# Two thirds of each down projection as seven products for eight, with sums of weights and activations on VectorE

## The reference, cut to what matters

```python
def swiglu(x, w_gate, w_up, w_down):
    return (jax.nn.silu(x @ w_gate) * (x @ w_up)) @ w_down
for l in range(DEPTH):                       # DEPTH = 2, D_FF = 2816, D_MODEL = 1024
    x = layer_norm(ALPHA * x + 0.5 * swiglu(x, ffn1...[l]), ...)
    x = layer_norm(ALPHA * x + mixer(x) @ w_out[l], ...)
    x = layer_norm(ALPHA * x + 0.5 * swiglu(x, ffn2...[l]), ...)
```

## Time and profile before

| | us |
|---|---|
| median of 3 runs | 3002.32 (3001.02 to 3002.56) |
| the profiled execution, span | 3005.2 |
| PE busy | 2914.0 (97%) |
| DVE busy | 1376.5 (46%) |
| ACT busy | 1024.2 (34%) |
| mean granted TensorE clock | 0.991 |

### The profile page before, as it was taken

The page is one execution under the profiler, slowest core; times in us unless marked ns, Lnnn a source line. Parts: engine busy times, 40 slices in busy tenths (PEclk is TensorE's granted clock), DMA queues, the critical chain, the costliest instruction groups (busy, mean ns, idle before and its releaser), DMA issues.

```text
span 3005.2 us, 34010 instructions
## 1 busy us (share of the span) xinstructions
PE 2914.0 (97%) x14625; PEld 2422.2 (81%) x14625; DVE 1376.5 (46%) x1931; ACT 1024.2 (34%) x1360; POOL 77.4 (3%) x91
## 2 busy tenths in 40 slices
PE   7999998999999989999999999999999999999998
PEld 7878887887888878888876888888888886788887
DVE  4345357734535663333556443334433364644235
ACT  4322443432234332222535422224222254542122
POOL 0010000001000000000100000000000100000000
PEclk9999999999999999999999999999999999999999
DMA  5222222322221222222521223232322351223222
GB/s 211 74 94 74 71 72 83 96 70 71 85 84 56 71 92 98 98 98 98 100 98 57 80 90 114 96 103 93 113 98 98 112 100 57 71 98 112 98 98 84
DMA packets 41318, 275.88 MB, mean 92 GB/s; under 512 B 5508, under 2 KB 5698, under 8 KB 9936
## 3 DMA queue, kind: packets, MB, share of 16 engines
q1 hardware_dynamic: 36064, 254.82, 25.0%
q0 software_dynamic: 4288, 15.22, 2.4%
q10 hardware_dynamic: 816, 3.67, 0.3%
HBM read 269.50 MB, written 2.10 MB: 90 GB/s over the span
## 4 chain that ended last, share of the span: by engine, by line
PE 91%; DVE 5%; ACT 2%; issue 1%; DMA 1%; DVEq 0%; ACTq 0%
PE G L395 16%; PE G L397 16%; PE G L396 16%; PE G L407 11%; PE G L409 11%; PE G L408 11%; DVE w_lo L1506 1%; PE A L902 1%; PE A L582 1%; PE A L924 1%; PE A L683 1%; PE A L912 1%; PE A L700 1%; DMA x<-in_x 1%; PE A L670 1%
## 5 line engine op out<-in xcount | busy, mean ns | idle before, releaser
L1506 DVE TENSOR_TENSOR w_lo<-raw,w_hi 128x2048 fp32r<-128x2048 f32 (+1 forms) x234 | 533.1, 2278 | 793.4 <-ACT w_hi L1006 792.9
L395 PE MATMUL G<-xT_hi,w_hi 128*128 128x512 f32 (+1 forms) x2368 | 881.0, 372 | 14.6 <-DVE x L2063 4.8
L397 PE MATMUL G<-xT_hi,w_lo 128*128 128x512 f32 (+1 forms) x2368 | 870.5, 368 | 0.0
L396 PE MATMUL G<-xT_lo,w_hi 128*128 128x512 f32 (+1 forms) x2368 | 869.8, 367 | 0.0
L1006 ACT ACTIVATE w_hi<-raw 128x2048 fp32r<-128x2048 f32 (+1 forms) x234 | 443.8, 1896 | 959.1 <-PE G L409 523.2
L395 PEld LDWEIGHTS G<-xT_hi,w_hi 128*128 128x128 f32 x2368 | 449.1, 190 | 87.0 <-DVE x L2063 5.2
L397 PEld LDWEIGHTS G<-xT_hi,w_lo 128*128 128x128 f32 x2368 | 448.9, 190 | 73.1
L396 PEld LDWEIGHTS G<-xT_lo,w_hi 128*128 128x128 f32 x2368 | 449.5, 190 | 68.8
L407 PE MATMUL G<-w_hi,h_hi 128*128 128x512 f32 x704 | 274.8, 390 | 1.0 <-DVE w_lo L1506 1.0
L409 PE MATMUL G<-w_hi,h_lo 128*128 128x512 f32 x704 | 274.0, 389 | 0.0
L408 PE MATMUL G<-w_lo,h_hi 128*128 128x512 f32 x704 | 273.9, 389 | 0.0
(11 more groups left out here) (297 smaller groups left out, 2984.1 us busy)
## 6 DMA issues: line engine op xcount, KB each, us to landing
raw<-in_stream SPq DMA_DIRECT2D x240, 1024.0 KB, 4.8
lnr<-in_ln_rows POOLq DMA_DIRECT2D x6, 1024.0 KB, 5.1
row<-in_rows POOLq DMA_DIRECT2D x6, 512.0 KB, 7.7
x<-in_x ACTq DMA_DIRECT2D x1, 2048.0 KB, 17.8
...
```

Source lines behind the costliest of these rows:

```text
L395: mm(o, a, hi[:, c, at:at + n], start=start and own_start, stop=False, **k)
L396: mm(o, a, lo[:, c, at:at + n], start=False, stop=False, **k)
L397: return mm(o, wl[:, col:col + P], hi[:, c, at:at + n], start=False, stop=stop, **k)
L1506: tt(w_lo[:, s, 0:nk, :], raw[:, r, 0:nk, :], w_hi[:, s, 0:nk, :].bitcast(F32), ALU.subtract).then_inc(lo_done, 1)
```

## The change

In each feed-forward the 11 units fall in parts of 4, 4 and 3. The down projections of the first two parts, 1024 hidden columns each, are no longer 4 tiles x 8 chunks x 2 halves. The 512 x 1024 activations and the 1024 x 1024 weights are taken as 2 x 2 quarters, and the result is made from seven products of quarters (256 tokens x 512 hidden x 512 outputs, 24 matmuls of 512 columns) in place of eight, in Winograd's form. Each product has a left side, h or one of four sums of h, and a right side, a quarter of the weights or one of four sums.

DVE makes the sums of h in each unit, in `work`, and ACT and DVE split them into `hs`, which has seven variants of 256 tokens. The quarters of weights are loaded by SP with alternate chunks (`alternate`, two loads of 0.5 MB each in 2 KB pieces), into the ring and a second buffer `raw2`; one quarter is loaded twice. DVE makes the sums of weights in place, two before the last unit's multiplications and two behind them. Then each of seven right sides is split like a block. The products go to banks 0 and 1, or 2 and 3, of G in turn; DVE adds each to `x` when it is done (`read_product`), and some accumulate upon the one before in the same bank.

In the last unit before the products ACT copies the block of product 0, then that of product 1, and then takes the two Silus; DVE subtracts both, makes two sums of weights, and then multiplies.

The third part of 3 units has 6 chunks, in blocks of 4 and 2 for each half, with new hand-written orders. The residuals of the norm before are done two in each of units 1 and 2. GpSimd's memset of `shift_t`, which now shares memory with `raw2`, waits for the first feed-forward's products.

```diff
-UNITS2 = 2 * (11 + 4) + 5 + 2
-FF_HALVES = ((6, (4, 4, 4)), (5, (4, 4, 2)))
-OUT2 = sum(2 * units + 2 * len(downs) for units, downs in FF_HALVES) + 10
+UNITS2 = 2 * (11 + 2) + 5 + 2
+SUMMED = 2
+LAST_DOWN = (4, 2)
+FF_HALVES = ((4, (4, 4)), (4, (4, 4)), (3, LAST_DOWN))
+FF_PARTS = tuple(units for units, _ in FF_HALVES)
+PRODUCTS = 7
+FF_BLOCKS = 2 * sum(FF_PARTS) + 4 * SUMMED + 2 * len(LAST_DOWN)
+OUT2 = FF_BLOCKS + 10
+SPLITS2 = BLOCK2 + 2 * SUMMED * (PRODUCTS - 4)
+RING2 = BLOCK2 - 2 * SUMMED * 2
+LEFT = (0, 1, 4, 3, 5, 6, 2)
+QUARTER = ((0, 0), (0, 0), (0, 1), (1, 1), (1, 1), (0, 1), (1, 0))
...
+        hs = sb("hs", [P, 4, 2, 7, 256], F32R, on=two)
+        with ExitStack() as over:
+            w3_hi = sb("w3_hi", [P, 2, BC], F32R, on=over)
+            w3_lo = sb("w3_lo", [P, 2, BC], F32R, on=over)
+        raw2 = sb("raw2", [P, 2, KB, BC], on=two)
...
+            def alternate(place, b, odd, signals):
+
+                for o in range(2):
+                    sp.dma_start(place[:, 2 * o:2 * o + 2, :],
+                                 stream[b + o:b + o + 1].rearrange("o p (k e n) -> (o p) k e n", e=2, n=BC)[:, :, odd, :]
+                                 ).then_inc(signals[o], 16)
+
+            def feed_forward(b, parts_before):
+
+                for n, units in enumerate(FF_PARTS):
+                    for i in range(2 * units):
+                        ring(b + i)
+                    b += 2 * units
+                    if n == SUMMED:
+                        for i in range(2 * len(LAST_DOWN)):
+                            ring(b + i)
+                        continue
+                    first = Q.split
+                    if parts_before + n == 0:
+                        sp.wait_ge(S["ln_c"], 1)
+                    alternate(raw2[:, 0], b + 2, 1, (raw2_in[0], raw2_in[0]))
+                    alternate(raw2[:, 1], b, 1, (raw2_in[1], raw2_in[1]))
+                    slot_free()
+                    alternate(raw[:, 0], b, 0, (half_in[0], raw_in[0]))
+                    taken(first + 4)
+                    slot_free()
+                    alternate(raw[:, 1], b + 2, 0, (half_in[1], raw_in[1]))
+                    taken(first + 3)
+                    sp.wait_ge(lo_done, first + 2 + 3)
+                    sp.wait_ge(S["w_sum"], 4 * (parts_before + n) + 4)
+                    alternate(raw2[:, 0], b + 2, 1, (raw2_in[0], raw2_in[0]))
+                    Q.split += PRODUCTS
+                    b += 4
...
+            def products(units):
+
+                for k in range(PRODUCTS):
+                    s, a = (Pos.off + Pos.turn) % 2, 2 * (k % 2)
+                    pe.wait_ge(lo_done, 2 * Pos.pair + Pos.off + 3)
+                    for i in range(2):
+                        if k < 2:
+                            pe.wait_ge(g_free[a + i], Pos.ubase + Pos.u + 1)
+                        else:
+                            pe.wait_ge(S["st_read"], N.st + 2 * (k - 2) + i + 1)
+                        o = G[:, a + i, :]
+                        for u in range(units):
+                            if i == 0:
+                                pe.wait_ge(S["ff_lo"], N.ff + 3 * u + min(k, 2) + 1)
+                            hi, lo = (hs[:, u, part, LEFT[k], i * P:i * P + P] for part in range(2))
+                            new, end = u == 0 and k in (0, 1, 3), u == units - 1
+                            mm(o, hi, w_hi[:, s, u, :], start=new, stop=False, skip_group_check=True)
+                            mm(o, hi, w_lo[:, s, u, :], start=False, stop=False, skip_group_check=True)
+                            last = mm(o, lo, w_hi[:, s, u, :], start=False, stop=end, skip_group_check=True)
+                        last.then_inc(blk_used if i else S["st_done"], 1)
+                    Pos.off += 1
+                N.st += 2 * PRODUCTS
+                Pos.held.update({0: N.st - 1, 1: N.st, 2: N.st - 3, 3: N.st - 2})
...
-            FF_ORDER = ((0, 0, 0, 4), (0, 1, 0, 4), (0, 2, 0, 4), (0, 3, 0, 4), (1, 0, 0, 4), (2, 0, 0, 2), (1, 1, 0, 4),
-                        (2, 1, 0, 2), (1, 2, 0, 4), (1, 3, 0, 2), (1, 3, 2, 4), (2, 2, 0, 2), (2, 3, 0, 2))
-            FF_LAST_ORDER = ((0, 0, 0, 4), (0, 1, 0, 4), (1, 0, 0, 4), (2, 0, 0, 2), (1, 1, 0, 4), (2, 1, 0, 2), (0, 2, 0, 4),
-                             (1, 2, 0, 4), (2, 2, 0, 2), (0, 3, 0, 4), (1, 3, 0, 4), (2, 3, 0, 2))
+            FF_ORDER = ((0, 0, 0, 4), (0, 1, 0, 4), (1, 0, 0, 2), (1, 1, 0, 2), (0, 2, 0, 4), (0, 3, 0, 2), (0, 3, 2, 4),
+                        (1, 2, 0, 2), (1, 3, 0, 2))
+            FF_LAST_ORDER = ((0, 0, 0, 4), (1, 0, 0, 2), (0, 1, 0, 4), (1, 1, 0, 2), (0, 2, 0, 4), (1, 2, 0, 2), (0, 3, 0, 4),
+                             (1, 3, 0, 2))
...
+
             def ffn(L, bias_rows=None):
-                for n, (units, downs) in enumerate(FF_HALVES):
+                for n, units in enumerate(FF_PARTS):
                     for u in range(units):
+                        before_products = n < SUMMED and u == units - 1
+                        if before_products:
+                            act.wait_ge(half_in[0], 16 * (N.parts + 1))
                         split()
+                        if before_products:
+                            act.wait_ge(raw2_in[1], 32 * (N.parts + 1))
+                            split_summed(raw2[:, 1])
+                        act.wait_ge(S["ff_lo"], N.ff)
                         for i in range(2):
 
                             done(i)
                             act.wait_ge(g_free[2 + i], Pos.ubase + Pos.u + 1)
                             fn(work[:, i * 512:i * 512 + 512], G[:, i, :], ACT.Silu).then_inc(g_free[i], 1)
-                        for i in range(2):
-                            act.wait_ge(g_free[2 + i], Pos.ubase + Pos.u + 2)
-                            fn(h_hi[:, 2 * u + i, :], work[:, 1024 + i * 512:1536 + i * 512],
+                        if n < SUMMED:
+                            act.wait_ge(g_free[2], Pos.ubase + Pos.u + 2)
+                            fn(hs[:, u, 0, 0, :], work[:, 1024:1280], ACT.Copy).then_inc(S["ff_hi"], 1)
+                            act.wait_ge(g_free[3], Pos.ubase + Pos.u + 2)
+                            fn(hs[:, u, 0, 1:3, :], work[:, 1536:2048].rearrange("p (a t) -> p a t", a=2),
                                ACT.Copy).then_inc(S["ff_hi"], 1)
-                        split()
+                            N.sums += 1
+                            act.wait_ge(S["ff_sum"], N.sums)
+                            fn(hs[:, u, 0, 3:7, :], work[:, 0:1024].rearrange("p (a t) -> p a t", a=4),
+                               ACT.Copy).then_inc(S["ff_hi"], 1)
+                            N.ff += 3
+                        else:
+                            for i in range(2):
+                                act.wait_ge(g_free[2 + i], Pos.ubase + Pos.u + 2)
+                                fn(h_hi[:, 2 * u + i, :], work[:, 1024 + i * 512:1536 + i * 512],
+                                   ACT.Copy).then_inc(S["ff_hi"], 1)
+                            N.ff += 2
+                        if not before_products:
+                            split(LAST_DOWN[1] if n == SUMMED and u == units - 1 else KB)
...
+                    if n < SUMMED:
+                        act.wait_ge(S["w_sum"], 4 * N.parts + 2)
+                        split_summed(raw2[:, 0])
+                        split_summed(raw[:, 1])
+                        act.wait_ge(S["w_sum"], 4 * N.parts + 3)
+                        split_summed(raw[:, 0])
+                        act.wait_ge(raw2_in[0], 32 * (2 * N.parts + 2))
+                        split_summed(raw2[:, 0])
+                        act.wait_ge(S["w_sum"], 4 * N.parts + 4)
+                        split_summed(raw2[:, 1])
+                        N.parts += 1
+                        Pos.fewer += PRODUCTS - 2
+                        split()
+                        split()
+                        Pos.end += PRODUCTS
                         continue
                     split()
...
+            def low_h(u, a, b, source):
+
+                N.ff += 1
+                dve.wait_ge(S["ff_hi"], N.ff)
+                tt(hs[:, u, 1, a:b, :], source.rearrange("p (a t) -> p a t", a=b - a), hs[:, u, 0, a:b, :].bitcast(F32),
+                   ALU.subtract).then_inc(S["ff_lo"], 1)
+
+            def sums_of_h(u):
+
+                dve.wait_ge(g_free[2], Pos.ubase + Pos.u + 2)
+                dve.wait_ge(g_free[3], Pos.ubase + Pos.u + 2)
+                h11, h21, h12, h22 = (work[:, 1024 + i * 256:1280 + i * 256] for i in range(4))
+                s1, s2, s3, s4 = (work[:, i * 256:i * 256 + 256] for i in range(4))
+                tt(s3, h11, h21, ALU.subtract)
+                link(tt(s1, h21, h22, ALU.add))
+                link(tt(s2, s1, h11, ALU.subtract))
+                tt(s4, h12, s2, ALU.subtract).then_inc(S["ff_sum"], 1)
+
+            def first_weight_sums():
+
+                ring_loads = 2 * Pos.pair + Pos.off - 2 - Pos.fewer
```

(59 more changed lines are left out.)

208 lines of the change are left out of this document (123 added, 85 removed).

## The result

The changed kernel takes 3078.27 us (median of four runs, 3073.72 to 3079.83) against 3002.44 for the kernel before (3001.02 to 3005.8): a ratio of 1.0244, 95% interval 1.0229 to 1.0258. It is 2.4% slower. The profiled execution has a span of 3078.0 us against 3005.2, so 72.8 us more in these two, and the granted clock was 0.975 against 0.991.

A forecast was written before the change was run, and what follows sets the result against it. TensorE, busy 2914 of 3005 us, was taken as the bound. 3005.2 - 43.5 + 92.8 + 19.5 + 3 = 3077.0 us span, with the median 2.9 below: 3074 us, 2.4% slower, range 3043 to 3103.

The forecast's parts named there:

- The order of work in a part: Last unit of a part: TensorE waits 2.8, 5.8 and 3.0 us; 11.6 us lost in each of eight parts, +92.8 us.
- T: The end of the last unit of a part, from which the prediction counted its steps.
- What was taken on trust: VectorE's sum of 2048 f32 columns costs what the subtraction costs, 2.29 us; bounds 2.1 to 2.5, 8 us in all.
- The slack of 0.9: Inside the products: the next block is ready 4.55 us after a product's end, while the following product lasts 5.44.
- The matmuls: Down projections of two parts in four feed-forwards: 192 matmuls fewer at 0.2267 us each, -43.5 us.
- The ends: Ends of the four feed-forwards: waits for the third block, the transposes and the tail, +19.5 us, bounds 8 and 28.
- gaps of 2.8, 5.8 and 3.0 at eight places: Sign to look for: TensorE idle that long behind the Silu, h's low part and a weight block's low part.
- The clock: After the 5.8 us gap in each part a fall to half speed costs 0.4 us, +3 us, bounds 0 and 14.
- X: The start of the last half of a feed-forward, from which the prediction counted the steps at its end.
- the clock stays low: Rival: half speed lasts through product 2, +2 to +5.4 us a part, 3090 to 3115 us; chance 0.12.
- Part of the chain only: Rival: the third gap in a part closes, or the ends are covered, 3030 to 3055 us; chance 0.12.
- Faster: Rival: product 1's copy doesn't hold the queue, each part loses 0.4 us, 2981 us; chance 0.04.

The follow-up runs named there:

- e1: The changed kernel with VectorE making the first two weight sums ahead of the subtraction of product 1's block: 3046.04 us.
- e3: The changed kernel with ScalarE's Silus and copies of h ahead of product 1's copy, and three weight sums ahead of VectorE's multiplications: 2992.81 us.
- e9: The kernel before with 256 of 2816 hidden columns left out of each feed-forward's down projections, 192 matmuls fewer: 2975.24 us.
- e2: The changed kernel with Silus and copies of h ahead of product 1's copy, and all four weight sums behind the unit's low parts: 3072.84 us.
- e7: The kernel of e2 with 30 unused matmuls added between products 1 and 2, 240 in all: 3053.57 us.
- e4: The changed kernel with the third block copied, subtracted and used in another order at the feed-forwards' ends only: 3070.44 us.
- e6: e3 plus e4, tiles 0 and 1 measured before the next block's low part, one weight sum on GpSimd, product 1's copy moved earlier: 2976.18 us.

## Why the prediction was right, step by step

**The order of work in a part (+92.8): right, and shown to be the cause.** Counted from T: ACT's copy 0.3 to 2.2, measured 0.28 to 2.19; PE starts at 2.8, measured 2.78; DVE's low part at 2.25, sums at 4.5 and 6.7, multiplications at 9.0, measured 2.23, 4.43, 6.82, 9.03; PE resumes at 10.7, measured 10.70; low part of product 2's block over at 22.45, measured 22.38, and in each of the eight parts 22.37 or 22.38. That is 11.5 us a part, 92 in all. e1 and e3 took 32 and 85 us away by order alone. Up to the next unit's first matmul a part takes 49.8 us, 11.7 more than its 168 matmuls are.

**What was taken on trust:** a sum of 2048 columns takes 2.28 to 2.29 us, as the subtraction does. Products 3 to 6 keep 5.44: ACT's later copies in the part shown are 5.44 us apart, and DVE waits 1.32 us for each, so it is not DVE that sets the pace. The slack of 0.9 held in spite of the reload (the loads of 0.5 MB landed in 6.2 us, the median of all 80). DVE's low parts of the later products:

```profile
1219.94 2.29 DVE L2286 TENSOR_TENSOR w_lo<-raw,w_hi 128x2048 fp32r<-128x2048 f32 x1 [1.32 <-ACT w_hi L1453]
...
1230.82 2.29 DVE L2286 TENSOR_TENSOR w_lo<-raw,w_hi 128x2048 fp32r<-128x2048 f32 x1 [1.32 <-ACT w_hi L1453]
```

**The matmuls (-43.5): the price was right** (e9's first part), and the count too. In the changed kernel the 120 matmuls from product 2 on take 27.3 us up to the next unit's first, 0.228 each.

**The ends (+19.5): right at each end, but not as the gaps that were to be seen.** With 11.7 us for each part, the stages leave 5.8, 4.5, 5.8 and 5.4 us for the ends of L = 0, 2, 3 and 5, where 5.9, 3.1, 5.9 and 4.5 stood; what is over in L=2 and L=5 is the clock, below. The waits for the third block came as counted, 2.6 to 2.7 us where 2.7 and 2.8 stood, and the transposes' wait in L=2 too, 3.45 for 3.6. In L=5 DVE became the bound of the tail as counted: it starts on the four tiles 5.04 us apart (3055.19 to 3070.32). In L=0 and L=3 the transposes' wait was 0.9 and 0.8 us for 3.8. DVE and ACT had not been faster: behind the 2.67 us gap ahead of it the clock was at half, the matmuls took some 3 us longer, and PE arrived later at a wait whose end was fixed. The end of the wait is what was predicted. This holds for the gap of 5.8 us too: in two parts the nine matmuls ran at full clock and it reads 5.60, in the six others it is 4.4 on average ((37.5 - 11.2) / 6). And it holds for the third of 3.0, which shows as 1.3 or less in five parts and not at all in three. So "gaps of 2.8, 5.8 and 3.0 at eight places" was wrong as a thing to look for, where "PE starts at T+2.8, T+10.7 and T+22.5" was right. DVE was busy for 1626 us where 1645 stood.

**The clock (+3): the size held by luck, its place did not.** The term put 0.4 us in each of eight parts. In all eight product 3 starts 5.5 to 5.6 us behind product 2: nothing of it came there. It came at two ends, where the term had nothing. The windows of the transposes in L=2 and of the third block's first matmuls in L=5, each behind a wait:

```profile
2076.70:2080.00 3.30, 3.29 (x16) 3.29 (x17) 0.46 (x1) 2.14 (x5) 0.00 (x0) 0.51 0.00 0
3052.50:3055.20 2.70, 2.67 (x7) 2.13 (x8) 0.01 (x1) 0.00 (x0) 0.00 (x0) 0.59 0.00 0
```

The transposes of L=2 take 3.3 us up to the next matmul, where those of L=0, at full clock, take 1.7. In L=5 DVE starts on the first tile at X+8.2, where X+7.1 stood (X is 3047.0), and as DVE bounds the tail, all of that goes into the time. That is 1.6 + 1.1 = 2.7 us.

In the parts the fall was covered. By its granted clock the kernel spent 154 us at half clock (2 x 0.025 x 3078) against 54 before (2 x 0.009 x 3005). 100 us more at half clock would be at most 50 lost, if nothing stood behind; as far as the stages show, 2.7 were. e2 and e7 are the proof that the cover does this: with no wait behind the gap, such a fall costs 2.1 to 2.4 us a part. The Trainium skill ("TensorE: Matmul & The Clock Gate", HAM oscillation) describes stretches that start cold after each idle wait; the trace agrees that they do, in most parts (0.56 behind the gap of 2.59 us shown, 1.00 behind the same gap in the part at 1792.5), and adds that this made no difference to the time in the parts, since another engine set the end.

The rival "the clock stays low" (3090 to 3115) is excluded: product 2 ran at 1.00 in the part shown and took 5.5 to 5.6 us in all eight, since the stretch at half clock was over before it. "Part of the chain only" is excluded too: no term failed to appear. "Faster" was a question of one copy that held the queue; e3 comes nearest to that rival, and it gives 2993 with the ends left as they are, against the 2981 worked out; 10 of the 12 us between them are the 1.3 us a part told under e3.

**What is left,** 4 us between 3074 and 3078, is made of +0.8 and +0.4 in L=2 and L=5 (the clock), -0.7 each in L=0 and L=3 (where the clock's 0.75 did not come), and 1.3 outside the feed-forwards; the other part is that four runs had a median at the span and not 2.9 below it, as those of before had. The last two can't be told from the scatter of the runs.

**Where my experiments' expectations failed:** e2 (the clock counted as free where its cover had been taken away), e4 (just outside its range: one of two orders left), e6 (the rival came true, with another mechanism: a narrow instruction waited, not the wide ones longer), e9 (the ends don't follow).
